# Feed-forward chunks with gate and up weights as the stationary operand

## What is computed

```python
def swiglu(h, wg, wu, wd):
    return (jax.nn.silu(h @ wg) * (h @ wu)) @ wd

y = swiglu(rms_norm(x, g[4]), ffn_wg[layer], ffn_wu[layer], ffn_wd[layer])   # first block
x = x + rms_norm(y, g[5])
x = x + 0.5 * swiglu_2(rms_norm_2(x, ffn1_norm[l]), ffn1_w1[l], ffn1_w3[l], ffn1_w2[l])   # second block
```

## Time and profile before

| | |
|---|---|
| median of 3 runs | 2120.72 us (2118.64 to 2123.4) |
| the profiled execution | 2119.11 us |
| its span, first to last instruction | 2117.2 us |
| TensorE busy | 2033.5 us (96%), 9948 matmuls |
| VectorE busy | 1252.6 us (59%) |
| ScalarE busy | 1043.3 us (49%) |
| mean granted TensorE clock | 0.978 |

### The profile page before, as it was taken

The page is one execution under the profiler, slowest core; times in us unless marked ns, Lnnn a source line. Parts: engine busy times, 40 slices in busy tenths (PEclk is TensorE's granted clock), DMA queues, the critical chain, the costliest instruction groups (busy, mean ns, idle before and its releaser), DMA issues.

```text
span 2117.2 us, 26909 instructions
## 1 busy us (share of the span) xinstructions
PE 2033.5 (96%) x9948; PEld 1675.8 (79%) x9948; DVE 1252.6 (59%) x1869; ACT 1043.3 (49%) x1680; POOL 146.9 (7%) x146
## 2 busy tenths in 40 slices
PE   7998899999879999999999999999999999999999
PEld 7775678887768888888778788888888877878887
DVE  5546654566765456545666865546554685775544
ACT  5545554455564445344556555435434556555443
POOL 0000000000010000000312200000000222120000
PEclk9987999999999999999999999999999999999999
DMA  8430365554236555555562545655555553435652
GB/s 289 125 112 11 128 205 185 193 188 153 67 118 199 182 191 175 192 181 178 153 202 88 179 139 179 193 184 180 193 185 188 170 184 119 159 121 179 196 181 100
DMA packets 247673, 346.13 MB, mean 163 GB/s; under 512 B 26164, under 2 KB 180088, under 8 KB 247544
## 3 DMA queue, kind: packets, MB, share of 16 engines
q1 hardware_dynamic: 246712, 342.92, 50.1%
q0 software_dynamic: 544, 1.29, 0.3%
q10 hardware_dynamic: 288, 0.21, 0.0%
HBM read 343.32 MB, written 2.33 MB: 163 GB/s over the span
## 4 chain that ended last, share of the span: by engine, by line
PE 88%; DVE 6%; ACT 3%; issue 2%; POOL 1%; DMA 0%; DVEq 0%; ACTq 0%; POOLq 0%
PE bank L666 26%; PE bank L668 26%; PE bank L667 26%; PE bank L942 2%; DVE w_lo L495 2%; PE bank L1070 1%; PE bank L1262 1%; PE bank L601 1%; ACT w_hi L507 1%; PE bank L1120 1%; POOL gain L2390 1%; PE bank L2047 1%; PE bank L1402 1%; DVE probs L1055 1%; DVE gain L1089 0%
## 5 line engine op out<-in xcount | busy, mean ns | idle before, releaser
L495 DVE TENSOR_TENSOR w_lo<-raw,w_hi 128x2048 fp32r<-128x2048 f32 (+5 forms) x491 | 743.0, 1532 | 421.5 <-ACT w_hi L507 421.2
L666 PE MATMUL bank<-w_hi,h_hi 128*128 128x512 f32 (+3 forms) x1904 | 747.2, 392 | 17.1 <-DVE w_lo L495 7.9
L507 ACT CAST w_hi<-raw 128x2048 fp32r<-128x2048 f32 (+5 forms) x491 | 620.3, 1291 | 265.0 <-PE bank L668 263.5
L668 PE MATMUL bank<-w_hi,h_lo 128*128 128x512 f32 (+3 forms) x1904 | 733.2, 385 | 0.0
L667 PE MATMUL bank<-w_lo,h_hi 128*128 128x512 f32 (+3 forms) x1904 | 732.8, 385 | 0.0
L666 PEld LDWEIGHTS bank<-w_hi,h_hi 128*128 128x128 f32 x1904 | 361.5, 190 | 90.9 <-DVE w_lo L495 5.5
L668 PEld LDWEIGHTS bank<-w_hi,h_lo 128*128 128x128 f32 x1904 | 361.1, 190 | 69.6
L667 PEld LDWEIGHTS bank<-w_lo,h_hi 128*128 128x128 f32 x1904 | 361.9, 190 | 63.9
L666 PE MATMUL bank<-w_hi,ff_hi 128*128 128x512 f32 x528 | 206.3, 391 | 0.0
L668 PE MATMUL bank<-w_hi,ff_lo 128*128 128x512 f32 x528 | 205.6, 389 | 0.0
L667 PE MATMUL bank<-w_lo,ff_hi 128*128 128x512 f32 x528 | 205.5, 389 | 0.0
(11 more groups left out here) (299 smaller groups left out, 1643.0 us busy)
## 6 DMA issues: line engine op xcount, KB each, us to landing
raw<-in_ffn_w SPq DMA_DIRECT2D x176, 512.0 KB, 4.7
raw<-in_w_in SPq DMA_DIRECT2D x48, 1024.0 KB, 5.3
raw<-in_ffn_w SPq DMA_DIRECT2D x44, 1024.0 KB, 4.9
raw<-in_ffn_wg SPq DMA_DIRECT2D x44, 512.0 KB, 4.0
raw<-in_ffn_wu SPq DMA_DIRECT2D x44, 512.0 KB, 5.0
raw<-in_ffn_wd SPq DMA_DIRECT2D x22, 1024.0 KB, 4.8
raw<-in_od_w_in SPq DMA_DIRECT2D x12, 1024.0 KB, 5.2
raw<-in_w_out SPq DMA_DIRECT2D x8, 1024.0 KB, 5.1
```

The source lines that it names most:

```text
L495: dve.tensor_tensor(lo_[:, cs], raw_[:, cs], hi[:, cs].bitcast(F32), ALU.subtract).then_inc(*dve_did.up())
L507: act.copy(hi[:, cs], raw_[:, cs]).then_inc(*act_did.up())
L666: pe.matmul(out, x_hi, u.hi[:, k, cols_], start=start, stop=False)
L668: return pe.matmul(out, x_lo, u.hi[:, k, cols_], start=False, stop=stop)
```

## The change

Chunks 1 to 10 of each feed-forward are computed with the weights stationary: `gate_up_turned` loads a 128 x 128 square of the gate or up weights and moves all 256 tokens past it. The output has hidden features on the partitions and tokens along the row, one bank for gate and one for up, which is the layout that `down` wants. So `hidden` and `transposes` go for these chunks; chunk 0 is as before. A token's scale is now different along a row and the same for all partitions. `spread_rstd` writes it once per call as a row over all partitions: two matmuls of the broadcast scale column with the identity, and a copy into `r_row` (in the buffer `qT`). `hidden_scaled` multiplies gate and up by this row on VectorE, with ScalarE's Silu between; `hidden_split` multiplies the two and splits the product into `ff_hi` and `ff_lo`. In chunk 10 `hidden_split` stands ahead of `take` and `down(9)`, in the others behind `down`.

```diff
--- before.py
+++ after.py
@@ -1251,6 +1251,113 @@
                                                  ff_silu[:, c % 2, tt, :], ALU.mult, ALU.mult).then_inc(*dve_did.up())
                     hid_done[(c, tt)] = bank.drained = dve_did.now()
 
+            r_row = qT[:, 0, :]
+            rows_of = r_row.unsqueeze(1).broadcast_to([P, KB, T])
+            row_there = {}
+
+            def spread_rstd():
+
+                bank = acc[-1]
+
+                @block.tensor
+                def _(pe):
+                    pe.wait_ge(*bank.drained)
+                    for tt in range(TT):
+                        pe.wait_ge(*turn["normed"][tt])
+                    for tt in range(TT):
+                        m = pe.matmul(bank.t[:, tt * P:(tt + 1) * P], r(tt).broadcast_to([P, P]), ident,
+                                      start=True, stop=True)
+                    m.then_inc(*pe_did.up())
+
+                @block.scalar
+                def _(act):
+                    act.wait_ge(*pe_did.now())
+                    act.copy(r_row, bank.t[:, 0:T]).then_inc(*act_did.up())
+                bank.drained = row_there["act"] = act_did.now()
+
+            def gate_up_turned(c, u, k0):
+
+                @block.tensor
+                def _(pe):
+                    if k0 == 0:
+                        for bank in pair[c % 2]:
+                            pe.wait_ge(*bank.drained)
+                    pe.wait_ge(*u.parted)
+                    for k in range(u.shape[0]):
+                        for m, bank in enumerate(pair[c % 2]):
+                            for b in range(KB):
+                                cs = slice(m * FF_CHUNK + b * P, m * FF_CHUNK + (b + 1) * P)
+                                out_ = bank.t[:, b * T:(b + 1) * T]
+                                pe.matmul(out_, u.hi[:, k, cs], h_hi[:, k0 + k, :], start=(k0 + k == 0 and b == 0),
+                                          stop=False, skip_group_check=True)
+                                pe.matmul(out_, u.lo[:, k, cs], h_hi[:, k0 + k, :], start=False, stop=False,
+                                          skip_group_check=True)
+                                mm = pe.matmul(out_, u.hi[:, k, cs], h_lo[:, k0 + k, :], start=False,
+                                               stop=(k0 + k == KD - 1), skip_group_check=True)
+                    mm.then_inc(*pe_did.up())
+                u.used = pe_did.now()
+
+            def by_block(v, c):
+
+                return v[:, c % 2, :, :].rearrange("p t n -> p (t n)").rearrange("p (b n) -> p b n", b=KB)
+
+            scaled, silued = {}, {}
+
+            def hidden_scaled(c):
+
+                full = pe_did.now()
+                gate_bank, up_bank = pair[c % 2]
+                gated, hid = by_block(ff_silu, c), by_block(ff_hid, c)
+
+                @block.vector
+                def _(dve):
+                    dve.wait_ge(*full)
+                    dve.wait_ge(*row_there["act"])
+                    if c == 1:
+                        dve.wait_ge(*before.act)
+                        dve.wait_ge(*before.pool)
+                    if c == 2:
+                        dve.wait_ge(*turned[0])
+                    dve.tensor_tensor(gated, gate_bank.t[:, :].rearrange("p (b n) -> p b n", b=KB), rows_of,
+                                      ALU.mult).then_inc(*dve_did.up())
+                gate_bank.drained = dve_did.now()
+
+                @block.scalar
+                def _(act):
+                    act.wait_ge(*dve_did.now())
+                    act.activation(gated, gated, ACT.Silu).then_inc(*act_did.up())
+                silued[c] = act_did.now()
+
+                @block.vector
+                def _(dve):
+                    dve.tensor_tensor(hid, up_bank.t[:, :].rearrange("p (b n) -> p b n", b=KB), rows_of,
+                                      ALU.mult).then_inc(*dve_did.up())
+                up_bank.drained = scaled[c] = dve_did.now()
+
+            def hidden_split(c):
+
+                gated, hid = by_block(ff_silu, c), by_block(ff_hid, c)
+
+                @block.vector
+                def _(dve):
+                    dve.wait_ge(*silued[c])
+                    dve.wait_ge(*scaled[c])
+                    dve.tensor_tensor(hid, hid, gated, ALU.mult).then_inc(*dve_did.up())
+
+                @block.scalar
+                def _(act):
+                    act.wait_ge(*dve_did.now())
+                    if c >= 2:
+                        act.wait_ge(*down_done[c - 2])
+                    act.copy(ff_hi[:, c % 2, :, :], hid).then_inc(*act_did.up())
+
+                @block.vector
+                def _(dve):
+                    dve.wait_ge(*act_did.now())
+                    dve.tensor_tensor(ff_lo[:, c % 2, :, :], hid, ff_hi[:, c % 2, :, :].bitcast(F32),
+                                      ALU.subtract).then_inc(*dve_did.up())
+                split[c] = dve_did.now()
+
             def transposes(c):
                 bank = pair[c % 2][0]
 
@@ -1324,21 +1431,18 @@
                     prepare()
                 gate_up(0, first[1], KD // 2, [tt])
                 hidden(0, [tt])
-            for c in range(1, NF + 1):
-                if c < NF:
-                    gate_up(c, take(), 0)
-                if 1 <= c < NF:
-                    transposes(c - 1)
-                if c < NF:
-                    gate_up(c, take(), KD // 2)
-                    hidden(c)
+            for c in range(1, NF):
+                gate_up_turned(c, take(), 0)
+                if c == 1:
+                    transposes(0)
+                    spread_rstd()
+                gate_up_turned(c, take(), KD // 2)
+                hidden_scaled(c)
                 if c == NF - 1:
-                    u = take()
-                    down(c - 1, u, range(KB // 2))
-                    transposes(c)
-                    down(c - 1, u, range(KB // 2, KB))
-                elif c < NF:
-                    down(c - 1, take())
+                    hidden_split(c)
+                down(c - 1, take())
+                if c < NF - 1:
+                    hidden_split(c)
             if following is None:
                 u = take(pieces=PIECES)
                 for tt in range(TT):
```

## The result

| | before | after |
|---|---|---|
| median of the runs | 2119.76 us (2118.64 to 2123.4) | 2136.28 us (2134.23 to 2137.08) |
| ratio to before | | 1.0071, 95% interval 1.0059 to 1.0083 |
| span of the profiled execution | 2117.2 us | 2134.6 us |
| TensorE busy | 2033.5 us | 2046.0 us |
| a chunk in the steady part | 16.80 us | 16.98 us |

Both medians are over four runs. The ratio on record is worked out over the runs and is not the quotient of the two medians, which is 1.0078. The change makes the kernel 16.5 us slower, 0.7 to 0.8%. The forecast was 2132.9 us with a range of 2123 to 2146.

What follows compares the result with a forecast made beforehand. TensorE's instruction stream was taken as the bound. +38.4 - 28.8 + 1.3 + 1.3 = +12.2 us on the profiled 2119.1 gave 2131.3, plus 1.6 for the median: 2132.9 us, range 2123 to 2146.

Steps and rivals of the forecast that it cites:

- Gate and up, +38.4: Chunks 1 to 10: 12 256-wide matmuls replace 6 512-wide per k, paying a fixed 13 ns twice as often; +38.4 us.
- The first rival: Gate/up: the fixed 13 ns per matmul does not come twice, the +38.4 goes; 2094.5 us, chance 0.08.
- The second rival: Gate/up matmuls come at about 118 ns, result within 4 us of before; chance 0.06.
- The transposes, -28.8: Feed-forward: 60 transpose groups go, each having held TensorE for 0.48 us; -28.8 us.
- The fifth rival: Chunks: the transposes' 0.48 us returns as an interruption at the change from 512 to 256 columns; 2162 us, chance 0.03.
- The spread row, +1.3: Chunk 1 of each call: two added fp32 matmuls at 0.107 us each; +1.3 us, at most +2.7.
- The end of a call, +1.3: After chunk 10: TensorE waits about 0.66 us for x in the two calls with post-norm; +1.3 us.
- DVE, ACT and weight loads, 0: Inside chunks: VectorE and ScalarE work hides behind TensorE, and doubled weight loads keep up; no cost.
- The third and fourth rivals: Third: DVE/ACT late at call ends or chunk 1, +6 to +12 us, 0.10; fourth: weight loads lag, 2162 us, 0.05.
- Sum: Whole kernel: gate/up, transposes, spread row and call-end terms together; +12.2 us.

Runs made afterwards that it cites:

- e1: Kernel before, with only the 512-wide gate/up matmuls of chunks 1 to 10 cut into two 256-wide ones; 2157.62 us, ratio 1.0170.
- e2: Kernel before without the transposes of chunks 1 to 10, hidden split unturned (output differs); 2095.30 us, ratio 0.9876.
- e5: Changed kernel, but in chunk 10 `down(9)` takes its unit without rounding the next one ahead; 2144.26 us, ratio 1.0108.
- e8: Changed kernel run again unchanged, for a second profile and comparison; 2135.51 us, ratio 1.0073 to the kernel before.
- e4: Changed kernel, with 4 512-wide and 4 256-wide alternating matmuls per k instead of 12 narrow in chunks 2 to 9; 2129.52 us, ratio 1.0037.
- e6: As e4, but in each unit the 16 wide matmuls stand first and the 16 narrow ones behind; 2115.15 us, ratio 0.9975 to the kernel before.
- e3: Changed kernel with the spread row set to 1.0 by VectorE instead of two matmuls and a copy; 2132.16 us, ratio 1.0052.

## Why the prediction was right

**Gate and up, +38.4.** Right. The beat is 0.1200 us in the changed kernel, 96 in 11.52, as in the earlier trace rows, and e1 shows the term without the rest of the change (+37.2). The windows of e1 give 60 x 0.61 = 36.6 (17.41 for 16.80); the transposes take 0.43 instead of 0.49 among narrow matmuls, which takes some of the 38.4 back.

**The first rival** (no second fixed part, 2094.5 us) needed at most 117.5 ns per matmul by the prediction's text; its own 26.2 us over 480 k blocks make that 117.9. It fell with 120.0 either way. The Trainium skill, page "TensorE: Matmul & The Clock Gate", section "Back-to-back issue gap", puts the warm gap of an isolated matmul at N/2.4 + 2.5 ns, 109.2 at 256 columns. For this kernel's stream of fp32r matmuls with a weight load each, the trace does not agree: the distance is 120.0 at 256 columns and 226.7 at 512, which is N/2.4 + 13.3 ns in both cases. The second rival (118 ns) fell too.

**The transposes, -28.8.** Right for the steady chunks: 0.48 in each by e2. For all 60 groups e2 shows it less closely (-26.5 within the calls, -25.1 at the medians), because its own edit brings a wait for `ff_lo` in five calls, as told there. The changed kernel has no such wait, and its calls add up to within 0.6 us of the terms (see the sum). The fifth rival (not given back) falls; a little of it is there, 0.02 us per chunk, since `down` takes 5.46 instead of 5.44 behind narrow matmuls: +1.2 us that the sum did not have.

**The spread row, +1.3.** Too small by half. It cost 0.45 per call, 2.7 in all, the upper bound. The step that failed is the reading of the earlier trace rows: the 16 records there come from 8 matmuls (two directions, two pairs and two tiles in the loop at line 2618). A plain fp32 matmul leaves two records, as the 24 records for 12 matmuls of the row show. So 0.107 us is the price of a record, and a matmul costs twice that, 0.21 there and 0.22 in the row.

**The end of a call, +1.3.** The mechanism is right: the two waits of 0.67 us are there, with VectorE's queue as their cause (e5). Since 0.3 us of such waits was there before, one of them 0.16 in the earlier trace rows, the term is 1.3 - 0.3 = +1.0. The three calls with `add_half` wait for nothing, as forecast.

**DVE, ACT and weight loads, 0.** Right. `ff_lo` came at G + 7.66, and no wait for w_lo or ff_lo appeared within chunks. The third and fourth rivals fall.

**Sum.** With the terms as measured one by one: 38.4 + 1.2 - 28.8 + 2.7 + 1.0 = +14.5 us, where +12.2 was forecast. The forecast was low by the row (1.4) and by `down` (1.2), and high by 0.3 at the end of a call. TensorE's starts give 0.6 less than 14.5. From the first transposes to the last matmul of `down` the six calls take 1023.5 us together, and 1012.6 before; with the first half of chunk 1 (6 x 0.32) that is +12.9, where the terms inside the calls make 13.5. Of the 0.6, 6 x 0.06 = 0.4 is `transposes(0)`, which now stands among narrow matmuls; the rest was not located.

The medians differ by 16.5 (first comparison) and 14.9 (e8). The two profiled spans differ by 17.4: 12.9 + 1.0, then 2.15 that stood ahead of the first turned chunk already (286.32 - 283.85 - 0.32), and 1.4 in the later stages between the calls. For e8 the same account is 12.9 + 1.0 + 3.8 - 1.3 = 16.4. One program gives 2.15 and 3.8, 1.4 and -1.3 for the last two parts, so they vary from execution to execution. That they are the clock is argued from the windows, not isolated by a run.

## What to carry to other kernels

When TensorE sets the time, count its instructions and not only its columns. A layout that saves transposes can cost more than they did if it halves the width of the moving operand: 13 ns for each of 2880 added matmuls outweighed 60 groups of transposes. If a narrow form is needed, see which of its products share a stationary operand and can be joined into one wide matmul, and keep equal widths together; here this turned 0.7% slower into 0.25% faster.

Before a duration is taken from a grouped row, count the program's instructions against its records. And before work at a boundary is put off, look at what stands on the same queue when it is made up for.

## What the runs showed of the hardware

- Matmuls 512 and 256 wide in turn take 0.352 us a pair (e4); with 16 of each in a row it is 0.346 (e6, 5.53 us for 16 pairs). Over 48 chunks the order alone was worth 10.6 us.
- Four fp32 transposes cost 0.49 us among 512-wide matmuls (5.93 - 5.44) and 0.43 among 256-wide ones (6.19 - 5.76 in e1 and e3).
- In one stretch of the same program (130 to 160 us) the mean granted clock was 0.72, 0.66 or 0.60 from one execution to another, and what followed came up to 4 us later.
- A plain fp32 matmul of 128 columns costs 0.22 us and leaves two records; four transposes leave four.
- 5760 weight loads of 0.192 us each passed at one per 0.120 us, and no matmul stood idle behind them.
